# Two more tokens of a mixture-of-experts stage by gathered rows (108 instead of 106), with another order of the row products

## What is computed

```python
def peer_ffn(h, w_q, sub_k1, sub_k2, expert_u, expert_v):
    ...
    v1, i1 = lax.top_k(s1, PEER_TOPK)
    v2, i2 = lax.top_k(s2, PEER_TOPK)
    ...
    vals, pos = lax.top_k(cand, PEER_TOPK)
    experts = jnp.take_along_axis(cand_idx, pos, axis=-1)
    gates = jax.nn.softmax(vals, axis=-1)
    ...
        u = expert_u[ec]
        a = jnp.einsum('cd,chkd->chk', xc, u).astype(jnp.float32)
        w = (jax.nn.gelu(a) * gc).astype(xc.dtype)
        return jnp.einsum('chk,chkd->cd', w, expert_v[ec])
```

## Time and profile before

| | before |
|---|---|
| median of three runs | 1746.03 us |
| the profiled execution, its own time | 1749.67 us |
| span of the profiled execution | 1747.9 us |
| PE busy | 1721.6 us (98%) |
| DVE busy | 1096.3 us (63%) |
| POOL, ACT busy | 310.4 us, 240.9 us |
| moved by DMA | 439.64 MB |

### The profile page before, as it was taken

The page is one execution under the profiler, slowest core; times in us unless marked ns, Lnnn a source line. Parts: engine busy times, 40 slices in busy tenths (PEclk is TensorE's granted clock), DMA queues, the critical chain, the costliest instruction groups (busy, mean ns, idle before and its releaser), DMA issues.

```text
span 1747.9 us, 29485 instructions
## 1 busy us (share of the span) xinstructions
PE 1721.6 (98%) x11745; PEld 1470.2 (84%) x11745; DVE 1096.3 (63%) x2430; ACT 240.9 (14%) x600; POOL 310.4 (18%) x282
## 2 busy tenths in 40 slices
PE   8999999999999999999999999999999999999997
PEld 7887576986999999999999858699955978699953
DVE  4653524797557888899432442379974762379974
ACT  1016510111423111000000011111100001011100
POOL 0010000344324344445322200000000000000000
PEclk9999999999999999999999999999999999999999
DMA  7534243699999999999999645365444535355451
GB/s 280 191 122 169 73 145 121 243 354 384 413 417 415 416 414 399 410 411 416 416 417 418 255 204 191 116 222 169 169 168 169 169 124 191 119 169 169 169 172 69
DMA packets 76609, 439.64 MB, mean 252 GB/s; under 512 B 8566, under 2 KB 8656, under 8 KB 37840
## 3 DMA queue, kind: packets, MB, share of 16 engines
q1 hardware_dynamic: 42624, 305.15, 46.6%
q0 software_dynamic: 32592, 125.92, 18.4%
q10 hardware_dynamic: 1280, 6.96, 1.0%
HBM read 432.69 MB, written 5.24 MB: 251 GB/s over the span
## 4 chain that ended last, share of the span: by engine, by line
PE 81%; DMA 8%; DVE 7%; issue 3%; ACT 0%; POOL 0%; SPq 0%; DVEq 0%; POOLq 0%
PE ps L1156 16%; PE ps L942 14%; PE ps L549 10%; PE ps L934 9%; PE ps L595 7%; DMA arena<-u_rows,sparse_pairs 6%; PE ps L1194 4%; PE ps L634 3%; PE ps L507 3%; DVE arena L1932 2%; PE ps L795 2%; PE ps L844 2%; PE ps L808 2%; PE ps L955 1%; PE ps L1025 1%
## 5 line engine op out<-in xcount | busy, mean ns | idle before, releaser
L934 PE MATMUL ps<-xT,ring 128*128 128x150 f32 x2048 | 266.8, 292 | 0.5 <-ACT arena L1443 0.5
L942 PE MATMUL ps<-arena,ring 128*128 128x150 f32 (+1 forms) x2048 | 266.3, 292 | 0.9 <-DMA ring<-stream 0.9
L934 PEld LDWEIGHTS ps<-xT,ring 128*128 128x128 f32 x2048 | 262.5, 190 | 0.8 <-ACT arena L1443 0.7
L942 PEld LDWEIGHTS ps<-arena,ring 128*128 128x128 f32 x2048 | 262.2, 190 | 1.1 <-issue 1.1
L549 PE MATMUL ps<-ring,arena 128*128 128x512 f32 x416 | 181.4, 592 | 0.4 <-ACT arena L1507 0.4
L2063 DVE SCALAR_TENSOR_TENSOR arena<-arena,sparse_dots 128x1024 f32<-128x1024 f32 x105 | 134.7, 1283 | 72.6 <-DMA arena<-v_rows,sparse_pairs 66.6
L1932 DVE CUSTOM_DVE_ANT_0 arena<-arena 128x1024 f32<-128x1024 f32 x107 | 128.1, 1222 | 73.6 <-DMA arena<-u_rows,sparse_pairs 73.2
L2538 POOL DMA_INDIRECT arena<-v_rows,sparse_pairs x107 | 133.7, 1249 | 224.7 <-DVE arena L2063 182.8
L2501 POOL TENSOR_SCALAR stat<-stat 128x1 f32<-128x1 f32 (+2 forms) x23 | 4.4, 192 | 895.0 <-DVE stat L2237 694.8
L2538 POOL DMA_INDIRECT arena<-u_rows,sparse_pairs x107 | 131.3, 1227 | 163.8 <-DVE sparse_dots L1932 139.6
L549 PEld LDWEIGHTS ps<-ring,arena 128*128 128x128 f32 x416 | 78.0, 190 | 93.0 <-issue 92.3
(11 more groups left out here) (345 smaller groups left out, 2203.3 us busy)
## 6 DMA issues: line engine op xcount, KB each, us to landing
ring<-stream SPq DMA_DIRECT2D x288, 1024.0 KB, 7.7
arena<-second_params POOLq DMA_DIRECT2D x6, 1024.0 KB, 5.3
arena<-kv_scratch POOLq DMA_DIRECT2D x2, 2048.0 KB, 14.0
kv_scratch<-arena ACTq DMA_DIRECT2D x2, 1024.0 KB, 10.8
arena<-held_params ACTq DMA_DIRECT2D x1, 2048.0 KB, 16.6
arena<-u_rows,sparse_pairs POOLq DMA_INDIRECT x107, 15.6
arena<-v_rows,sparse_pairs POOLq DMA_INDIRECT x107, 13.4
arena<-second_params POOLq DMA_DIRECT2D x1, 1536.0 KB, 6.5
```

Source lines behind the costliest of these rows:

```text
L934: ins = pe.matmul(ps[:, o % 2, 0:DENSE], w[:, (o % 2) * D + k * P:(o % 2) * D + (k + 1) * P], xT[:, k, 0:DENSE], start=(k == 0), stop=(k = ...
L942: ins = pe.matmul(ps[:, 4 + k // 2, c:c + DENSE], w[:, (o % 2) * D + k * P:(o % 2) * D + (k + 1) * P], H[:, n, :], start=first and k % 2 = ...
```

## The change

`SPARSE_C` = 2 further tokens (148 and 149) go by rows: 64 partitions each, two pairs per partition, so two more chunks of `u` and two of `v` (109 each); `DENSE` falls from 150 to 148. Their token values are spread to 128 partitions by one ACT copy, 8 transposes on PE between the `v1` and `k0b` sections, and two ACT copies; four small DMAs on POOL's queue bring their indices and gates; the fold has 8 more matmuls. The last set of gates has 4 tokens instead of 6. The order of the row work has other constants. The core of the diff:

```diff
-SPARSE = SPARSE_A + SPARSE_B
+SPARSE_C = 2
+SETS_B, SETS_C = P // SPARSE_B, P // SPARSE_C
+SPARSE = SPARSE_A + SPARSE_B + SPARSE_C
...
-CHUNKS = PAIRS_HALF + PAIRS_B
+FIRST_C = PAIRS_HALF + PAIRS_B
+PAIRS_C = P // SETS_C
+CHUNKS = FIRST_C + PAIRS_C
...
-DOTS_SCORES = (5, 5, 5, 4, 4)
+DOTS_SCORES = (6, 6, 6, 6, 6)
...
-DOTS_SUMS = (4, 4, 4, 4, 3)
-DOTS_PICK = 3
-DOTS_FIRST = 73
-DOTS_TURN = 77
-TURNS_UP = 119
-TURNS_DOWN = 167
+DOTS_SUMS = (2, 2, 2, 2, 2)
+DOTS_PICK = 2
+DOTS_FIRST = 76
+DOTS_TURN = 79
+TURNS_UP = 122
+TURNS_DOWN = 171
...
-WEIGH_GROUP = 7
+WEIGH_GROUP = 5
...
+            pe.wait_ge(x_last_wide, 1)
+            pe.wait_ge(xres_T_ready, 4)
+            for k in range(KT):
+                ins = pe.transpose(ps[:, 2 + k // 4, (k % 4) * P:(k % 4 + 1) * P], x_wide_c[:, k], ident)
+            ins.then_inc(x_last_psum, 1)
...
-                for part, (name, n) in enumerate((("fold", SPARSE_A), ("fold_b", SPARSE_B))):
-                    c = (k % 2) * T + (T - SPARSE_A, DENSE)[part]
-                    ins = pe.matmul(ps[:, 4 + k // 2, c:c + n], sparse_sum[:, part, k * P:(k + 1) * P], sm(name),
+                for part, (name, n) in enumerate((("fold", SPARSE_A), ("fold_b", SPARSE_B), ("fold_last", SPARSE_C))):
+                    c = (k % 2) * T + (T - SPARSE_A, DENSE + SPARSE_C, DENSE)[part]
+                    ins = pe.matmul(ps[:, 4 + k // 2, c:c + n], row_sums[part][:, k * P:(k + 1) * P], sm(name),
...
+            act.wait_ge(x_sparse_ready, 1)
+            act.copy(x_wide_c.rearrange("p k (t e) -> p k t e", e=SETS_C),
+                     xT[:, :, DENSE:DENSE + SPARSE_C].unsqueeze(3).to_broadcast([P, KT, SPARSE_C, SETS_C]))\
+                .then_inc(x_last_wide, 1)
...
                 if m == PAIRS_HALF:
-                    pool.wait_ge(pairs_in, 16 * (3 + SETS_B))
+                    pool.wait_ge(pairs_in, 16 * (3 + SETS_B + 2 * SPARSE_C))
...
+                    for t in range(SPARSE_C):
+                        for n in range(2):
+                            pool.dma_start(pairs[SETS_C * t:SETS_C * (t + 1), n, FIRST_C:],
+                                           pairs_out_b[c_first + t:c_first + t + 1, n, 0:P]
+                                           .rearrange("o (e m) -> o e m", e=SETS_C)).then_inc(pairs_in, 16)
```

More of the change, by code:

```diff
@@ L41 @@
 SPARSE_B = 42
-SETS_B = P // SPARSE_B
-SPARSE = SPARSE_A + SPARSE_B
+SPARSE_C = 2
+SETS_B, SETS_C = P // SPARSE_B, P // SPARSE_C
+SPARSE = SPARSE_A + SPARSE_B + SPARSE_C
 DENSE = T - SPARSE
@@ L67, with set_of @@
 U_FIRST = 96
+def set_of(m):
+    return 0 if m < PAIRS_HALF else 1 if m < FIRST_C else 2
 def u_fetch(m):
@@ L150 @@
                   ("cmp_b1", 4), ("cmp_b2", 2 * HEAD), ("pool_scale", 4), ("sgu_b", 4),
-                  ("ffn_conv", 2 * FT * 4), ("c_conv", KT * 3), ("fold", HEAD), ("fold_b", SPARSE_B),
+                  ("ffn_conv", 2 * FT * 4), ("c_conv", KT * 3), ("fold", HEAD), ("fold_b", SPARSE_B), ("fold_last", SPARSE_C),
                   ("fold_c", CG)]:
@@ L216, in build @@
         H_WORDS = EXPERT_BLOCKS * DENSE
-        ARENA = H_WORDS + (ROWS + 4) * D + KT * T + KT * T
+        ARENA = H_WORDS + (ROWS + 5) * D + KT * T + KT * T
         arena = sb("arena", [P, ARENA])
@@ L315, in build @@
         fetched = a3.take(ROWS * D).rearrange("p (b n) -> p b n", b=ROWS)
-        x_sparse = a3.take(2 * D).rearrange("p (s n) -> p s n", s=2)
+        x_sparse = a3.take(3 * D).rearrange("p (s n) -> p s n", s=3)
         sparse_sum = a3.take(2 * D).rearrange("p (s n) -> p s n", s=2)
         x_wide = sparse_sum[:, 1, :].rearrange("p (k n) -> p k n", k=KT)
+        x_wide_c = sparse_sum[:, 0, :].rearrange("p (k n) -> p k n", k=KT)
+        row_sums = [sparse_sum[:, 0, :], sparse_sum[:, 1, :], x_sparse[:, 2, :]]
         xres_T = a3.take(KT * T).rearrange("p (k t) -> p k t", k=KT)
@@ L412, in build @@
         x_wide_ready = sem("x_wide_ready")
+        x_last_wide, x_last_psum, x_last_ready = sem("x_last_wide"), sem("x_last_psum"), sem("x_last_ready")
         dot_gelu_b, weight_b_ready = sem("dot_gelu_b"), sem("weight_b_ready")
@@ L968, in _ @@
                 up_turn(m, 8, 0, m)
-            pe.wait_ge(xres_T_ready, 4)
+            pe.wait_ge(x_last_ready, 1)
             for n, i in enumerate(TILES):
@@ L1428, in _ @@
             spill_second(3, mT.rearrange("p k t -> p (k t)"))
+            act.wait_ge(x_last_psum, 1)
+            for q in range(2):
+                ins = act.copy(x_sparse[:, 2, q * 512:(q + 1) * 512], ps[:, 2 + q, :])
+            ins.then_inc(x_last_ready, 1)
             for c in range(4 - K0_FIRST):
@@ L1463, in _ @@
             act.wait_ge(sel_ready, 2)
-            act.wait_ge(pairs_in, 16 * (3 + SETS_B))
+            act.wait_ge(pairs_in, 16 * (3 + SETS_B + 2 * SPARSE_C))
             with act.Fori(HALF_BLOCKS // 2, HALF_BLOCKS // 2 + WEIGH_AT) as n:
@@ L2053, in row_adds @@
                 for m in range(adds_done[0], adds_done[0] + count):
-                    f, part = v_fetch(m), m // PAIRS_HALF
+                    f = v_fetch(m)
                     b = f % ROWS
                     dve.wait_ge(row_in[b], 16 * (f // ROWS + 1))
-                    total = sparse_sum[:, part, :]
-                    if m % PAIRS_HALF == 0:
+                    total = row_sums[set_of(m)]
+                    if m == 0:
+                        dve.wait_ge(x_last_ready, 1)
+                    if m in (0, PAIRS_HALF, FIRST_C):
                         dve.tensor_scalar(total, fetched[:, b, :], dots[:, 0, m:m + 1], None, ALU.mult)\
@@ L2118, in _ @@
                     if hf == 0 and g == WEIGH_GROUP:
-                        dve.wait_ge(pairs_in, 16 * (3 + SETS_B))
+                        dve.wait_ge(pairs_in, 16 * (3 + SETS_B + 2 * SPARSE_C))
                         weigh(slice(0, PAIRS_HALF), dot_gelu, weight_ready)
@@ L2541, in fetch @@
                     bounds_check=EXPERT_BLOCKS * P - 1, oob_is_err=True).then_inc(row_in[b], 16)
-            b_first = T - SPARSE - P
+            c_first = T - SPARSE - P
+            b_first = c_first + SPARSE_C
             def fetch_u(m):
@@ L2717, in _small @@
     put("fold_b", np.concatenate([np.eye(SPARSE_B)] * SETS_B + [np.zeros((P - SETS_B * SPARSE_B, SPARSE_B))]))
+    put("fold_last", np.repeat(np.eye(SPARSE_C), SETS_C, axis=0))
     put("fold_c", np.concatenate([np.eye(CG)] * (P // CG)))
```

6 lines of the change are left out of this document (3 added, 3 removed).

## The result

The change is slower, by half a per cent. Six executions of it took 1749.02 to 1761.09 us, median 1754.24; six of the kernel before beside them 1743.43 to 1749.26, median 1746.72. The ratio is 1.0050, with a 95% interval of 1.0033 to 1.0066: 5.8 to 11.5 us. Forecast was 1745.0, range 1738.0 to 1750.5. The profiled execution took 1751.33 us (span 1749.5); before it was 1749.67 (span 1747.9).

What follows compares the result with a forecast made beforehand. PE, busy 98% of the span, was taken as the bound, with DMA engines also full from 420 to 952 us. PE's terms of -7.3 us plus 6.3 us of returning waits gave -1.0: 1745.0 us, range 1738.0 to 1750.5.

Steps and rivals of the forecast that it cites:

- Columns: Expert matmuls on PE: 4096 records lose 2 of 150 columns, saving 6.8 us (bounds 6.0 to 7.0).
- The wait at L974: PE's 2.46 us wait before a transpose goes, with 0.5 us for ACT: 2.9 us saved.
- Gate sets, transposes: Last gate set of each half, 8 matmuls instead of 12, saves 0.2 to 0.3 us; 8 more transposes cost 0.9 us.
- The new wait: PE at gate sets and the start of `mixed(0)` waits for chunks to land: 6.3 us come back.
- the idle DMA time: Unused 6 and 4 GB/s in the two mixed stretches would be used, bringing 1.4 MB or 2.7 chunks.
- The fold: 8 more matmuls, 16 records of 2 columns at 0.109 us each, cost PE 1.75 us (bounds 0 and 1.75).
- Beside it: ACT copies, DVE's four further products and additions, and four small DMAs lie beside PE's path and add no time.
- The cover before `residual`: DVE's 23.86 us wait for PE before `residual` shrinks to some 5 to 15 us but is not used up.
- Rival 2: Idle DMA time is not won back; waits 9.7 to 10.4 us, time 1748.4 to 1749.1, up to 1751.7; chance 0.13.
- Rival 1: Chunks keep up at 8 GB/s more, returning waits under 2 us, time 1738.7 to 1740.8; chance 0.27.

Runs made afterwards that it cites:

- order_first73: Kernel before with the change's products between the search steps and gating at set 5, but its own 73 chunks and turns: ratio 0.9985 to the kernel before.
- fold_wide: Changed kernel with the third fold table widened from 2 to 64 columns, 62 of them zeros: ratio 1.0022 to the kernel before.
- fold_none: Changed kernel without the 8 fold matmuls (16 records) of the two further tokens, whose sums miss the output: ratio 1.0013 to the kernel before.
- group7: Changed kernel with the gating of the first rows before set 7 instead of set 5 of `mixed(0)`: ratio 1.0039 to the kernel before.
- turn76: Changed kernel with DOTS_TURN 76 instead of 79, so fewer turns before the gate sets of `mixed(0)`: ratio 1.0023 to the kernel before.
- first70: Changed kernel with the 64-column fold table, 70 instead of 76 chunks before `sel16` and turns from 73 instead of 79: ratio 1.0019 to the kernel before.
- balance14: Changed kernel, fold table and 24-column records widened to 64, 73 chunks before `sel16`, turns 76 to 120 to 169, 14 additions behind the residual, gating at set 7: 1.0017.
- best106: Kernel before (106 tokens by rows) with order_first73's constants and the 24-column records near 85 us widened to 64: ratio 0.9985, median 1742.83 us.
- first66: Changed kernel with the 64-column fold table, 66 chunks before `sel16`, turns from 69 to 119 to 169: ratio 1.0051 to the kernel before.
- order106: Kernel before (106 tokens by rows) with all order constants of the change and nothing of the two tokens: ratio 1.0034 to the kernel before.

## Why the prediction was wrong, point by point

- **Columns.** Right: 126.0 instead of 127.75 ns in the pure down stretch, 7.1 us for 4096 records (6.8 forecast; just above the upper bound of 7.0).
- **The wait at L974.** Right: gone, with the 0.5 us for ACT. order_first73, which takes it away with four of the order's constants and without the two tokens, gained 0.7 to 4.5 us (2.9 forecast).
- **Gate sets, transposes.** Right: 0.40 us for 8 matmuls, 0.87 us for the transposes from 411.49 to 412.36 us.
- **The new wait.** Near in size, if only its length counts: 6.3 us forecast; 6.0 in the change, 5.8 in fold_wide, 6.1 in fold_none, 5.2 in group7, but 9.4 in turn76. Part of that is luck. The sum was worked out for the late sets of `mixed(1)`, with 3 us of it at the start of `mixed(0)`; most came at the start, at `sel16` or a set later, and 0 to 2 us in `mixed(1)`. In the change PE lost 8.7 us at set 1, so that its late sets had no wait left, and the sum was not put to the test there. The landing times that it reads to a tenth of a us vary by 8 us (turn76). And the idle DMA time that was to bring 2.7 chunks did not come in the change: it moved 403 and 415 GB/s in the two mixed stretches, some 115.1 MB, against 410 and 412, some 115.7 MB, before. In fold_wide, at 414 against 411 GB/s over both stretches together, some of it did.
- **The price of that wait: the first step that failed.** I charged a wait with its own length. In the change 48 records behind it took 8.59 instead of 6.29 us and 16 small ones 1.03 instead of 0.63: the 6.03 us cost 8.7. The granted clock of 0.72 and 0.59 behind the wait is what the forecast left out. It does not fall behind every wait, as fold_none shows:

```profile
573.10 0.64 PE L970 MATMUL ps<-e 128*128 128x64 f16 x16 [3.35 <-DVE e L2124]
573.57 6.29 PE L949 MATMUL ps<-xT,ring 128*128 128x148 f32 x48
```

- **The fold: the second.** "Something else sets their pace, and I let the new ones of 2 columns count the same", 1.75 us with that as its upper bound. They cost 3.8 us in the fold (7.26 against 3.50) and 1.3 in the 64 records behind it (8.50 against 7.22): 5.1 us. fold_wide, at 0.110 us a record, shows that the price of a record was right and the clock was what it left out.
- **Beside it.** The cover before `residual` came out as forecast (10.2 us, 5 to 15). `WEIGH_GROUP`, which the diff shows, I left without a cost; its 6.2 us of DVE cost PE nearly nothing in the profile.

In place of the sum: -7.1 - 2.9 - 0.2 + 0.9 + 5.1 + 8.7 = +4.5 us. From the first record of the expert matmuls (428.5 us before, 426.2 after) to the end of the span the two profiled executions took 1319.4 and 1323.3 us; with the transposes, which lie ahead of that, the difference is 3.9 + 0.9 = 4.8 us. So the two clock terms turn the forecast -1.0 into some +4.5 us. The median is 7.5 us above. Some 2 us of the rest go with the clock again, by the same estimate as above: the profiled execution has 0.994, the mean of the six 0.9928. Where the clock fell in the five others no trace shows; that part stays open.

Rival 2, the slower one, came nearest in time (1751.7 at most) with another mechanism, DMA time that is not won back. It was not won back in the change, but the waits were 6.0 us and not rival 2's 9.7 to 10.4; the low clock was in no rival. Rival 1 is refuted for this split: in none of the eleven profiles with 108 tokens did PE's waits stay under 2 us, and the 8 GB/s more that it needed are in none of the change's stretches up to 845 us (415, 403 and 415 GB/s).

What stays open: whether some order makes 108 tokens pay. The best of mine, first70 and balance14, are at 1.0019 and 1.0017, best106 at 0.9985.

## What to carry to other kernels

Where PE and the DMA engines are both full, time taken from PE comes back as a wait; moving the deadline moves the wait. A wait of a busy PE can cost more than its length: look at the granted clock behind it, and at every run of narrow matmuls, where padding with zero columns can make the program faster. And test an order's constants one by one: here a gain and a loss stood in the same edit.

## What the runs showed of the hardware

- The granted clock can fall to 0.50 while PE is busy all the time: in the fold (16 of 48 records with 2 columns), and behind 32 records of 24 columns, there in 5 of 12 profiles with the same instructions at that place. With 64 columns it stayed at 1.00 in both places (three profiles of the fold, four of the other), unless PE had waited just before the fold: behind 1.4, 1.9 and 1.4 us it fell in two of three.
- Behind PE's waits it fell too: 3.46 us were followed by a stretch at 0.50, 6.03 by 0.72 and 0.59, 8.00 by 0.52 and 0.50; the 2.46 us of before were not. The length of the wait alone does not decide it: 3.35 us in fold_none and 2.22 in turn76 were followed by 1.00, 2.38 us in first66 by 0.66. The Trainium skill ("TensorE: Matmul & The Clock Gate", section "HAM oscillation — how this bites in real kernels") says that gaps in PE's work put it back to the lower clock, at which the next matmuls start. The trace of order106 agrees, with 16 records in 4.37 instead of some 2.1 us behind 3.46 us of waiting. The first point, a fall without a gap, is not covered by that sentence.
